# Gate columns of the input projection moved from matmuls of their own into the first value group, and the groups of a head reordered

## The reference, cut to what matters

```python
n1 = rmsnorm(x, norm_mix_g)
proj = n1 @ w_in                       # 2048 x 6152
q, k, v, o_pre, if_pre, x_r, g_r = split(proj)   # 4 x 1024, then 8, then 2 x 1024
i_pre, f_pre = if_pre + b_gate         # 4 heads each: the gate columns
h_m = mlstm_chunkwise(q, k, v, i_pre, f_pre)     # 4 heads x 256, cumulative log-forget, running max
h_m = sigmoid(o_pre) * rmsnorm_per_head(h_m)
h_r = rglru(conv4(x_r)) * gelu(g_r)    # 8 blocks x 128
x = x + concat(h_m, h_r) @ w_out       # 2048 x 2048
gate, up = split(rmsnorm(x) @ w_up)    # 2048 x 11264
x = x + (silu(conv3(gate)) * up) @ w_down        # 5632 x 2048
return rmsnorm(x, norm_final_g)
```

## Time and profile before

| | |
|---|---|
| median of 3 runs | 1137.47 us (1136.65 to 1137.6) |
| span of the profiled execution | 1135.8 us |
| TensorE busy | 1125.2 us, 99% |
| VectorE busy | 749.2 us, 66% |
| ScalarE busy | 578.7 us, 51% |
| GpSimd busy | 51.6 us, 5% |
| DRAM traffic | 213.56 MB, mean 188 GB/s |

### The profile page before, as it was taken

One profiled execution on the slowest core, in us unless ns is written; L12 is line 12 of the kernel. 1 busy time (PEld: TensorE's weight loads), 2 busy tenths in 40 slices (PEclk: granted clock), 3 DMA queues, 4 the chain that ended last, 5 costly groups with the idle time before them and its releaser, 6 DMA issues.

```text
span 1135.8 us, 18132 instructions
## 1 busy us (share of the span) xinstructions
PE 1125.2 (99%) x6030; PEld 968.0 (85%) x6030; DVE 749.2 (66%) x989; ACT 578.7 (51%) x768; POOL 51.6 (5%) x48
## 2 busy tenths in 40 slices
PE   9999999999999999999999999999999999999997
PEld 8888888888888888888888888888888888888886
DVE  6768576595776686666666666766666655556554
ACT  6656464564665664344434444443544545555454
POOL 0100100100000000000000000000000000002000
PEclk9999999999999999999999999999999999999999
DMA  8756657657555466656665665666566565655653
GB/s 265 226 161 186 191 150 205 167 166 194 183 199 196 153 185 206 190 161 215 191 184 173 211 190 165 204 201 186 167 208 195 190 196 190 194 192 186 196 190 114
DMA packets 166617, 213.56 MB, mean 188 GB/s; under 512 B 6940, under 2 KB 149532, under 8 KB 166464
## 3 DMA queue, kind: packets, MB, share of 16 engines
q1 hardware_dynamic: 165456, 210.40, 60.2%
q0 software_dynamic: 560, 2.24, 0.6%
q10 hardware_dynamic: 576, 0.60, 0.2%
HBM read 211.10 MB, written 2.11 MB: 188 GB/s over the span
## 4 chain that ended last, share of the span: by engine, by line
PE 95%; DVE 3%; ACT 1%; issue 0%; DVEq 0%; ACTq 0%
PE ps L1066 41%; PE ps L1190 27%; PE ps L1068 20%; PE ps L1062 3%; PE ps L1064 1%; DVE w L612 1%; PE ps L1161 0%; PE ps L1041 0%; DVE aT L618 0%; ACT w L351 0%; PE ps L1084 0%; PE ps L1113 0%; PE ps L1143 0%; PE ps L1133 0%; DVE xT L663 0%
## 5 line engine op out<-in xcount | busy, mean ns | idle before, releaser
L1066 PE MATMUL ps<-xT,w 128*128 128x512 f32 x2048 | 716.7, 396 | 1.0 <-DVE w L678 0.5
L612 DVE TENSOR_TENSOR w<-raw,w 128x1024 fp32r<-128x1024 f32 x391 | 479.1, 1237 | 342.9 <-ACT w L351 341.9
L351 ACT ACTIVATE w<-raw 128x1024 fp32r<-128x1024 f32 (+1 forms) x393 | 409.7, 1055 | 417.2 <-PE ps L1068 247.6
L1068 PE MATMUL ps<-xT,w 128*128 128x256 f32 x2048 | 569.2, 278 | 0.0
L1066 PEld LDWEIGHTS ps<-xT,w 128*128 128x128 f32 x2048 | 384.2, 188 | 91.1 <-DVE w L612 1.0
L1068 PEld LDWEIGHTS ps<-xT,w 128*128 128x128 f32 x2048 | 385.2, 188 | 0.2
L1190 PE MATMUL ps<-w,aT 128*128 128x512 f32 x1440 | 327.9, 389 | 0.9 <-DVE aT L618 0.9
L1190 PEld LDWEIGHTS ps<-w,aT 128*128 128x128 f32 x1440 | 269.8, 188 | 57.6 <-DVE aT L618 1.7
L351 ACT ACTIVATE fs<-fc 128x512 f32<-128x512 f32 x22 | 13.9, 632 | 101.0 <-DVE fc L962 101.0
L1025 POOL TENSOR_TENSOR fs<-fs,rB 128x512 f32<-128x512 f32 x22 | 28.4, 1293 | 569.5 <-ACT fs L351 569.5
L1062 PE MATMUL ps<-w,xT 128*128 128x512 f32 x128 | 45.2, 398 | 0.0
(11 more groups left out here) (147 smaller groups left out, 391.8 us busy)
## 6 DMA issues: line engine op xcount, KB each, us to landing
raw<-w_up_dram SPq DMA_DIRECT2D x176, 512.0 KB, 4.6
raw<-w_in_dram SPq DMA_DIRECT2D x95, 512.0 KB, 3.9
raw<-w_down_dram SPq DMA_DIRECT2D x88, 512.0 KB, 4.6
raw<-w_out_dram SPq DMA_DIRECT2D x32, 512.0 KB, 4.6
xres<-x_dram SPq DMA_DIRECT2D x3, 512.0 KB, 7.8
y_dram<-xn SPq DMA_DIRECT2D x3, 384.0 KB, 3.1
bc<-rows POOLq DMA_DIRECT2D x4, 256.0 KB, 6.9
gfin<-gfin_dram POOLq DMA_DIRECT2D x1, 1024.0 KB, 4.6
```

The lines of the kernel that those rows point to most:

```text
L351: return sc.activation(out_, in_, fn, **kw)
L612: v.tensor_tensor(w[:, s, :, 1, :], raw[:, s, :].rearrange("p (c n) -> p c n", c=CH), w[:, s, :, 0, :], ALU.subtract).then_inc(lo_ready, 1)
L1066: mm(full, w[:, s, c, 0, cut], xT[:, kt, :, :].rearrange("p a n -> p (a n)"), start=kt == 0, stop=False)
L1068: ins = mm(rest, w[:, s, c, 1, cut], xT[:, kt, 0, :], start=False, stop=kt == KT - 1)
```

## The change

The ring `w` gets rows of 272 instead of 256 columns (`WROW`). In the 16 spare columns behind each high part stand, once at the start, the gate columns of that tile of the contraction: 8 high and 8 low. The first group is now V of head 0, with `gated=True`: each pair of matmuls becomes three, of 272, 256 and 264 moving columns, whose outputs all land at the start of a PSUM bank, so that value and gate columns are summed there. The sixteen gate matmuls, `gws` and its clearing go. The gate sums come out with positions as rows; ScalarE scales them (`gtok`), VectorE adds the two parts (`gpad`), and two transposes on TensorE bring them into rows of gates, behind the first unit of the Q group. The groups begin V, Q, K; a head is O, XR, GR and then V, Q, K of the next head, and the scores move behind the second unit of O. The load of the gate columns (`gw`) moves from GpSimd's queue to ScalarE's, third of four there, and its rounding on ScalarE from between units 2 and 3 of group 0 to the front of the first transposed tile.

```diff
+WROW = COLS + 4 * 4
...
-        w = sb("w", [P, RING, CH, 2, COLS], F32R)
+        w = sb("w", [P, RING, CH, 2, WROW], F32R)
...
             act_e.dma_start(ident, const_in[:, C_ID:C_ID + P]).then_inc(ident_landed, 16)
+            act_e.dma_start(gw[:], gate_w).then_inc(gate_landed, 16)
             act_e.dma_start(par[:, PAR_GMIX + KT:], par_in[:, PAR_GMIX + KT:]).then_inc(par_landed, 16)
             after(act_e, V0, "start")
             warm_sqrt(A0)
+            act_e.wait_ge(gate_landed, 16)
+            did(act_fn(w[:, :, :, 0, COLS:COLS + 2 * H].rearrange("p s c n -> p (s c) n"), gw[:].rearrange("p k a h -> p k (a h)")), A0, "gw_hi")
             act_e.wait_ge(gain_landed, 16)
             transposed_hi(A0, E0, PAR_GMIX, 0)
...
-            after(act_e, E0, "gates")
-            did(act_fn(grow[:], ps[0:64, B_SC, 0:S]), A0, "gate_half")
-            copy_half(0, 0, qT[:])
-            round_units(1, [2])
...
+            after(act_e, V0, "rstd1")
+            values(0)
+            for r in range(ROWS):
+                ins = act_fn(gtok[:, r, :], ps[:, r, COLS:WROW], scale=small[:, RSTD + r:RSTD + r + 1])
+            ins.then_inc(half_copied, 1)
+            round_units(1, [2, 3])
...
-            did(v.memset(gws[:].bitcast(F32), 0.0), V0, "gw_zero")
+            v.memset(gpad[:], 0.0)
+            after(dve, A0, "gw_hi")
+            w_gate = w[:, :, :, 0, COLS:WROW].rearrange("p s c n -> p (s c) n")
+            did(v.tensor_tensor(w_gate[:, :, 2 * H:4 * H], gw[:].rearrange("p k a h -> p k (a h)"), w_gate[:, :, 0:2 * H], ALU.subtract), V0, "gw_lo")
...
             split_units(1, [1])
+            dve.wait_ge(half_copied, 1)
+            v.tensor_tensor(gpad[:, :, :, 0:H], gtok[:, :, 0:2 * H].rearrange("p r (a h) -> p r a h", a=2),
+                            gtok[:, :, 2 * H:4 * H].rearrange("p r (a h) -> p r a h", a=2), ALU.add).then_inc(group_free, 1)
+            split_units(1, [2, 3])
             row_scales(V0, E0)
...
+                        if gated:
+                            for part, high, end in ((0, 0, WROW), (1, 0, COLS), (0, 1, COLS + 2 * H)):
+                                ins = mm(ps[:, 2 * pair + n, 0:end], xT[:, kt, high, cut], w[:, s, c, part, 0:end],
+                                         start=kt == 0 and part == 0 and high == 0, stop=kt == KT - 1 and high == 1)
...
-            after(pe, V0, "gw_lo")
-            for kt in range(KT):
-                ins = mm(ps[:, B_SC, :], gws[:, kt, :, :].rearrange("p a n -> p (a n)"),
-                         xT[:, kt, :, :].rearrange("p a n -> p (a n)"), start=kt == 0, stop=kt == KT - 1)
-            did(ins, E0, "gates")
-            spread_rows(V0, E0)
             pe.wait_ge(group_free, 2)
             for s in range(RING):
                 unit(1, s, 1)
-                if s == 2:
+                if s == 0:
+                    spread_rows(V0, E0)
+                    pe.wait_ge(group_free, freed(0))
+                    for r in range(ROWS):
+                        ins = nc.tensor.transpose(ps[0:64, B_SC, r * P:(r + 1) * P], gpad[:, r, :, :].rearrange("p a h -> p (a h)"), ident)
+                    did(ins, E0, "gates")
+            pe.wait_ge(group_free, 3)
+            for s in range(RING):
+                unit(2, s, 0)
+                if s == 0:
                     after(pe, V0, "gdif")
...
-                group(g0, g0, 0, rows_out=True)
...
+                pe.wait_ge(group_free, g0 + 1)
+                for s in range(RING):
+                    unit(g0, s, 1)
+                    if s == 1:
+                        after(pe, V0, "gcol1")
+                        pe.wait_ge(group_free, freed(g0 - 1))
...
                 if not last:
-                    group(g0 + 4, g0 + 4, 0)
-                    group(g0 + 5, g0 + 5, 1)
+                    group(g0 + 3, g0 + 3, 0, rows_out=True)
+                    group(g0 + 4, g0 + 4, 1)
+                    group(g0 + 5, g0 + 5, 0)
```

More of the change, by code:

```diff
@@ L170, in hybrid_block @@
         gates = ExitStack()
+        gtok = sb("gtok", [P, ROWS, 4 * H], where=gates)
+        gpad = sb("gpad", [P, ROWS, 2, F_ROW], where=gates)
         grow = sb("grow", [64, S], where=gates)
@@ L219, in hybrid_block @@
         rows = "rstd0 rstd1 diag0 diag1 rB "
[L220 to L223, removed]
+        A0 = Steps(act_step, 0, "warm gw_hi t0 t1 sq0_0 sq1_0 t2 t3 t4 t5 t6 t7 sq0_1 sq1_1 sq1_2 std0 std1"
+                   " lam_exp f_exp f_ln lam_ln floor")
+        V0 = Steps(dve_step, 0, "start gw_lo " + early + "lam_neg lam_abs lam_relu half_bias hg t4 t5 t6 t7 base base1 "
+                   + rows + "gate_b f_neg f_abs rm0 rm1 tri0 tri1"
                    " logf fsum gdif cmax neg_M neg_m neg_clip softplus c_col nc_col gcol0 gcol1 pads")
-        E0 = Steps(pe_step, 0, early + late + "gates rB gcol0 gcol1")
+        E0 = Steps(pe_step, 0, early + late + "rB gates gcol0 gcol1")
         A1 = Steps(act_step, A0.end(), "decay hsq rms_std o_tanh r_tanh0 r_tanh1 i_tanh0 i_tanh1 lru_a0 lru_a1 lru_t0 lru_t1 lru_s g_tanh")
@@ L428, in _ @@
                 transposed_hi(A0, E0, PAR_GMIX, b)
[L429 to L433, removed]
+            round_units(0, [2, 3])
             for b in (6, 7):
@@ L700, in _ @@
                 transposed_lo(A0, V0, PAR_GMIX, b)
-            split_units(0, [2])
-            after(dve, A0, "gw_hi")
-            did(v.tensor_tensor(gws[:, :, 2:4, 0:H], gw[:], gws[:, :, 0:2, 0:H], ALU.subtract), V0, "gw_lo")
-            split_units(0, [3])
+            split_units(0, [2, 3])
             for b in (6, 7):
@@ L782, in head @@
                                     gcol[:, 1, bass.ds(i, 1)], 0.0, ALU.add, ALU.min), V1, "arg1")
-                dve.wait_ge(half_copied, g0 + 1)
-                for r in range(ROWS):
-                    ins = v.scalar_tensor_tensor(out=vN[:, r, :], in0=ps[:, r, COLS:2 * COLS], scalar=small[:, RSTD + r:RSTD + r + 1],
-                                                 in1=vN[:, r, :], op0=ALU.mult, op1=ALU.add)
-                ins.then_inc(group_free, 1)
+                split_units(g0 + 1, [0])
                 after(dve, L1, "mask", i)
@@ L880, in head @@
                 else:
-                    add_half(g0 + 4, 0, qT[:])
+                    dve.wait_ge(half_copied, g0 + (3 + 1))
+                    for r in range(ROWS):
+                        ins = v.scalar_tensor_tensor(out=vN[:, r, :], in0=ps[:, r, COLS:2 * COLS], scalar=small[:, RSTD + r:RSTD + r + 1],
+                                                     in1=vN[:, r, :], op0=ALU.mult, op1=ALU.add)
+                    ins.then_inc(group_free, 1)
+                    split_units(g0 + 5)
+                    add_half(g0 + 4, 1, qT[:])
                     split_units(g0 + 6)
-                    add_half(g0 + 5, 1, kT[:])
+                    add_half(g0 + 5, 0, kT[:])
             with dve.Fori(0, H - 1) as i:
@@ L1069, in part_of_unit, with unit @@
                 return ins
-            def unit(g, s, pair, rows_out=False, tiles=None):
+            def unit(g, s, pair, rows_out=False, tiles=None, gated=False):
                 pe.wait_ge(lo_ready, g * RING + (s + 1 + RING))
-                part_of_unit(s, pair, range(CH), rows_out, tiles).then_inc(unit_used, 1)
+                part_of_unit(s, pair, range(CH), rows_out, tiles, gated).then_inc(unit_used, 1)
             def group(g, n_banked, pair, rows_out=False):
```

169 lines of the change are left out of this document (78 added, 91 removed).

## The result

The changed kernel takes 1154.06 us (median of four runs, 1153.14 to 1154.89), the kernel before, measured beside it, 1137.53: a ratio of 1.0148, 95% interval 1.0135 to 1.016. It is slower by 16.5 us, where a gain of 3.2 us had been forecast. The profiled execution has a span of 1152.6 us beside 1135.8.

A forecast was written before the change was run, and what follows sets the result against it. TensorE's back-to-back instructions were taken to bound the kernel, so its saved work counts one for one: -3.67 + 0.22 + 0.22 = -3.2 us, from 1137.47 to 1134.2 us, range 1133.3 to 1136.0.

The forecast's parts named there:

- The ring's rows of 272: Contractions already read the ring in two runs of 256 columns at 0.228 us, so longer rows were priced at nothing.
- The fourth rival: New ring rows slow its reading: 2 ns on each of 1440 contraction matmuls, 2.9 us, giving 1137.1 us; chance 0.05.
- The gate matmuls and the triples: Sixteen gate matmuls go, -3.67 us; first-group pairs become triples, 0.011 us more each, +0.22 (bounds +0.2 and +1.0).
- The second rival: In the first group's triples the third weight load is exposed, 0.115 us each: 1137.2 us, no change; chance 0.05.
- the third: Rival: weight loads take their shown 0.19 us, a triple 0.56, net +2.8 us, so 1140.3 us; chance 0.03.
- the transposes of the gate sums: Two new TensorE transposes behind the Q group's first unit: +0.22 us, bounds 0 and 0.5.
- The tight places: Without the gate matmuls' 3.67 us other engines get less far ahead; still no new TensorE wait was expected.
- The K group's first unit: Tightest place: split ends at 35.7, TensorE wants it at 36.1, 0.4 us early; up to 1 us if short.
- the scores: Two units into O, 5.6 us behind K's end; K's second half needs 3.5 us, so no wait.
- The start: Gate load and `gw_hi` before ScalarE's first transposed tile, landing at 4.7 and hidden: 0 us, bounds 0 and +0.4.
- The sum: All terms together: -3.2 us, a span of 1132.6 and a time of 1134.2 us.

The follow-up runs named there:

- e1: Kernel before with only the ring's rows changed, 272 columns instead of 256, the 16 spare ones unused: 1155.81 us, ratio 1.0161.
- e4: Changed kernel with ring rows of 320 columns instead of 272, gate tiles sharing `mixT`'s room: 1135.77 us, ratio 0.9984 to the kernel before.
- e9: Kernel before with `xT` alone begun 64 bytes later, all else in place modulo 512 bytes: 1149.11 us, ratio 1.0101.
- e2: Changed kernel, but only its first group reads a ring with rows of 272, all else one with rows of 256: 1137.71 us, ratio 1.0001.
- e8: e4 with the scores one unit later, behind the third unit of O: 1135.04 us, ratio 0.9978 to the kernel before.
- e13: Kernel before with the ring begun 32 bytes further from `xT`, and `aT` 32 bytes further from the ring: 1156.74 us, ratio 1.0168.
- e12: Kernel before with 64 bytes ahead of the first tile, so every SBUF tile moves and distances stay: 1137.72 us, ratio 1.0001.
- e11: e8 with the gate columns' load issued ahead of the other loads on ScalarE's queue: 1135.39 us, ratio 0.9981 to the kernel before.
- e3: Kernel before with 2 KB of unused room between the ring and `aT`, the ring itself unchanged: 1137.11 us, ratio 0.9996.
- e10: Kernel before with `aT` alone begun 64 bytes later, all else in place modulo 512 bytes: 1155.81 us, ratio 1.0161.
- e6: Kernel before with ring rows of 288 columns (1152 bytes), gate tiles sharing `mixT`'s room: 1142.94 us, ratio 1.0052.
- e5: Kernel before, rows of 256, with the ring begun 64 bytes later and `aT` moved by 128: 1157.36 us, ratio 1.0176.
- e14: Kernel before with the ring begun 128 bytes further from `xT`, and `aT` 128 bytes further from the ring: 1152.68 us, ratio 1.0131.

## Why the prediction was wrong

**The step that failed** is "*The ring's rows of 272.* ... Priced at nothing". Its reason was that a read in two runs of 256 columns already went at the pace of one run. That row has two runs 2048 bytes apart, which keeps the operands' distance at a multiple of 256 bytes. It says nothing of a step of 1088 bytes, which doesn't. The text noticed it, "No row shows a stride at work", but only beside a rival. The term got no bounds, though no row shows its cost. What the runs showed in its place is a loss of 16.5 us in the changed kernel and of 18.4 in e1, where the rows are all that changed: some 6 ns more on each pair and on each contraction matmul, in stages whose instructions the change leaves as they were.

**The fourth rival was right in kind, but mis-sized and too narrow.** It let the new rows slow the reading of the ring. It is not the stride as such, as rows of 320 cost nothing (e4), nor the ring alone, as moving `xT` does it too (e9). It took 2 ns on 1440 contraction matmuls; measured are 134.09 - 130.60 over 576, 6.1 ns, so 8.7 us instead of 2.9. It left out the 1408 pairs of the up projection, which read the same ring as weights: 6.6 ns each, 9.3 us. A weight load was thought of as covered, so its speed was not asked for. The same text says that it turns slower from 4 ns on, and no row favoured 2 ns over 6; 0.05 was too small a chance for a cost without a row. e1 shows the whole loss with the rows alone, e2 no loss without them.

**The gate matmuls and the triples** came as forecast. L1113 is gone. The timeline of TensorE in the changed kernel:

```profile
8.70 1.70 PE L1067 MATMUL ps<-w,xT 128*128 128x272 f32 x12 [1.48 <-DVE w L687]
...
18.11 6.12 PE L1067 MATMUL ps<-w,xT 128*128 128x272 f32 x48
24.07 0.40 PE L1073 MATMUL ps<-xT,w 128*128 128x512 f32 x1
...
27.30 0.38 PE L1125 MATMUL ps<-cst,gpad 128*64 128x128 f32 x2
```

Sixteen triples take 24.07 - 18.11 = 5.96 us. The first matmul after transposes is 0.11 slower than a running one (0.23 against 0.12), so a triple takes 0.366, where 0.364 was forecast. The second rival, the third weight load exposed, and the third are out, and with them the rule of the Trainium skill ("TensorE: Matmul & The Clock Gate", "The mechanism") that weight loads overlap only across row groups: this trace disagrees with it, since 0.366 us hold 0.330 of columns and three loads, which take 0.115 each at their closest. The prediction names the section behind it. The same section also lets a load run ahead when it goes to a background weight buffer; this trace would agree with that. The group ended at 24.07 (24.1 forecast), and the transposes of the gate sums fit into 27.30 to 27.44, before the next wide matmul (0.2 forecast).

**The tight places.** The K group's first unit, with 0.4 us of slack, was in time: no wait of TensorE for it is listed, and the split that it wants ended at 34.45 + 1.13 = 35.58 (35.7 forecast). So the place named as most likely to wait didn't. The wait came at the scores instead. The working counted the engines' steps from K's last unit, 3.5 of 5.6 us, and took the load of the unit behind for landed. It was not: it took 9.30 us. Why it took so long isn't shown.

**The start.** ScalarE waited for the gate load until 5.99 and began its first tile 0.07 later than before:

```profile
5.99 0.31 ACT L352 ACTIVATE w<-gw 128x128 fp32r<-128x128 f32 x1 [1.81 <-DMA gw<-gate_w_dram]
6.20 0.82 ACT L352 ACTIVATE xT<-ps,par 128x256 fp32r<-128x256 f32 x2
```

So the load landed some 4.3 us after its issue at 1.70, not the 3.0 chosen for its size, and cost 0.04 (8.70 against 8.66). In e4 the load landed later still, and the chain of work runs through it to a first matmul at 9.30; in e8, with the same instructions there, it stands at 8.38. One execution doesn't give this term: in the kernels whose start is as before, without any gate load, the first matmul stands anywhere from 8.26 (e13) to 10.18 (e12). The same holds for the start of e11.

**The sum, with the ring put right.** Even so the forecast gain of 3.2 us is too large. The interval of e2, which is the change with a harmless ring, allows at most 0.9 us, and that of e4 0.7 to 2.8. Only e8 and e11 come near it (1.5 to 3.6 and 1.0 to 3.2), and they have the scores moved as well. In the profiled executions e2 reaches the output projection 1.4 us earlier than the kernel before (318.48 against 319.87), e4 2.6 and e8 4.6, but e3 and e12, whose heads are those of before, stand at 318.90 and 320.56. The terms of the sum for TensorE's own work came as forecast; what was priced at nothing took part of them back: the wait for `kT` (1.0 us in e4, 0.3 in e2), in some executions the start, and the pace of the heads, below. How the rest divides among them is open.

## What to carry to other kernels

Before an SBUF tile that TensorE reads all the time is widened, padded or moved, work out the distance between its rows and those of the other operand of each matmul, and keep it at a multiple of 256 bytes. (That 256 bytes are enough rests on the rows of 320, whose low parts lie an odd multiple of 256 off; a whole tile so placed was not run.) Here all seven kernels that did were fast (e8 and e11 have the layout of e4), and the nine that didn't lost 0.5 to 1.8%. A pad to the next such row (320 numbers instead of 272) costs only room. A change of layout is a change of every instruction that reads the tile, in every stage: count these, and where no row of the trace shows the new step, give it bounds instead of nothing. Six nanoseconds on each of 1408 pairs and 1440 matmuls outweigh sixteen matmuls saved.

## What the runs showed of the hardware that was not expected

**Distance between operands.** The table above: 6.6 ns on a pair for remainders of 32, 64 and 192 bytes and 4.4 for 128; 6.6 ns on a contraction matmul for 32 and 64 and 5.7 for 128. The common shift of e12 costs nothing. Why distance matters isn't shown. The next weight load runs beside the moving operand's read (PEld is 84% busy), so the two reads may get in each other's way; no run tests this. Nor is it explained why rows of 288 leave the pairs of the up projection alone (492.21) while a constant distance of 128 bytes doesn't (498.47). Two things on record bear on it. In rows of 288 all high parts keep a multiple of 256 bytes and only the low parts are 128 off. And in the heads of the same kernel the pairs do lose:

```profile
85.64 1.73 PE ps L1162 x8
...
123.77 0.86 PE ps L1134 x4
```

This stretch takes 38.13 us, and so do the next two of its kind. In the kernel before, the same stretch takes 37.78 or 38.47, which is the next point.

**Two paces of the same code.** Even with all distances right, the heads run at one of two paces. In the chain of the kernel before, from the eight L1161 matmuls of one head to the scores of the next:

```profile
85.50 1.73 PE ps L1161 x8
...
123.97 0.86 PE ps L1133 x4
...
158.75 1.73 PE ps L1161 x8
...
196.53 0.86 PE ps L1133 x4
```

The first stretch takes 38.47 us, the second 37.78 with the same instructions, and TensorE waits for nobody in either. From start to start the pairs of the first take 0.353 us and those of the second 0.347, the two values that distances make elsewhere; the pace changes only at the short matmuls between groups, and after that stays. e10 is the extreme case: its `xT` and ring lie as in the kernel before, and its whole up projection, which follows contractions at 0.2333, runs at the slow pace. The 9.35 us that it loses there may be a pace taken over from the stretch ahead and kept. This is argued, not shown, and two kernels speak for some caution: in e6 the contractions ahead are slower too (55.73 us for the 240, against 54.72) and the pairs of the up projection are fast, and in e9 slow pairs are followed by fast contractions (130.62). If it is so, some of the 9.3 us in the changed kernel, in e5, e13 and e14 may be of this kind too, and the prices of a pair above are those of a whole layout; e9 shows that a wrong distance between `xT` and ring makes the pairs slow behind fast contractions too. What sets the pace, and whether it can be held at the fast one in the heads, is open. It is worth 0.7 us in such a stretch. In the new order the stretch has more pairs; in the profiled execution of e2 all three run at the slow pace, 44.13 us like this one,

```profile
82.83 1.73 PE ps L1174 x8
...
126.96 0.86 PE ps L1148 x4
```

and in that of e4 one does (44.13) and two don't (43.33). That is 1.6 us between two kernels with the same instructions in the heads and no wrong distance there, so the first parts of e2, e4, e8 and e11 are comparable only within a microsecond or two.
